# First modulation products of a two-block model on one Trainium2 core: four column quarters of the TensorE array, and the latent tokens' modulation ahead of the context's norm

## What is computed

```
def adaln(cvec, w, b):
    m = jax.nn.silu(cvec) @ w + b
    return jnp.split(m, 3, axis=-1)
...
sh_l, sc_l, gt_l = adaln(c, ada_w[i], ada_b[i])
h_lat = rms_norm(x_lat, norm_g[i]) * (1.0 + sc_l[:, None]) + sh_l[:, None]
...
sh_c, sc_c, gt_c = adaln(c_ctx, ada_w[i], ada_b[i])
h_ctx = rms_norm(x_ctx, norm_g[i]) * (1.0 + sc_c) + sh_c
...
y_lat, y_ctx = hgrn_mixer(h_ctx, h_lat, hg_w_in[j], lb, hg_norm_g[j], hg_w_out[j], ctx_out)
```

## Time and profile before

| | |
|---|---|
| median of 3 runs | 2519.7 us (2518.5 to 2519.74) |
| the profiled execution | 2521.25 us, span 2518.5 us |
| PE busy | 2461.1 us (98%) |
| DVE busy | 1633.3 us (65%) |
| ACT busy | 993.6 us (39%) |
| mean granted TensorE clock | 0.992 |

### The profile page before, as it was taken

One profiled execution on the slowest core, in us unless ns is written; L12 is line 12 of the kernel. 1 busy time (PEld: TensorE's weight loads), 2 busy tenths in 40 slices (PEclk: granted clock), 3 DMA queues, 4 the chain that ended last, 5 costly groups with the idle time before them and its releaser, 6 DMA issues.

```text
span 2518.5 us, 40380 instructions
## 1 busy us (share of the span) xinstructions
PE 2461.1 (98%) x14398; PEld 2147.0 (85%) x14398; DVE 1633.3 (65%) x2378; ACT 993.6 (39%) x1338; POOL 120.3 (5%) x138
## 2 busy tenths in 40 slices
PE   7999999999999998999999999989999999999998
PEld 2888888888888886888899999979999878888886
DVE  7567777777777775445555343468999975444346
ACT  4334444444444433333345222235455554322223
POOL 0011211111111100000000000000000000000000
PEclk9999999999999998999999999999999999999999
DMA  6212212122121232222222222222222222222222
GB/s 239 78 64 75 75 67 75 58 76 82 67 67 64 78 126 75 83 76 83 85 92 91 88 88 92 92 84 92 100 97 94 100 84 97 95 92 92 99 92 100
DMA packets 61983, 223.90 MB, mean 89 GB/s; under 512 B 6736, under 2 KB 8784, under 8 KB 61552
## 3 DMA queue, kind: packets, MB, share of 16 engines
q1 hardware_dynamic: 58992, 211.08, 24.7%
q0 software_dynamic: 2944, 12.19, 1.4%
HBM read 221.15 MB, written 2.10 MB: 89 GB/s over the span
## 4 chain that ended last, share of the span: by engine, by line
PE 93%; DVE 4%; ACT 1%; issue 1%; DMA 1%; ACTq 0%; DVEq 0%; SPq 0%
PE ps L489 81%; PE ps L663 4%; PE ps L685 1%; PE ps L546 1%; DMA ada_raw<-in_ada_weights_dram 1%; PE ps L676 1%; PE ps L704 1%; PE ps L650 1%; PE ps L695 1%; PE ps L696 1%; PE ps L697 1%; ACT w_hi L1060 1%; DVE w_lo L1603 1%; PE ps L633 0%; DVE n_sq L1622 0%
## 5 line engine op out<-in xcount | busy, mean ns | idle before, releaser
L1060 ACT ACTIVATE w_hi<-w_raw 128x1024 fp32r<-128x1024 f32 (+1 forms) x360 | 377.8, 1049 | 922.5 <-PE ps L489 913.7
L1603 DVE TENSOR_TENSOR w_lo<-w_raw,w_hi 128x1024 fp32r<-128x1024 f32 (+1 forms) x360 | 435.3, 1209 | 214.4 <-ACT w_hi L1060 212.2
L489 PE MATMUL ps<-n_hi,w_hi 128*128 128x512 f32 (+1 forms) x992 | 320.5, 355 | 11.9 <-DVE n_lo L1630 8.5
L489 PE MATMUL ps<-n_lo,w_hi 128*128 128x512 f32 (+1 forms) x992 | 319.6, 354 | 0.0
L489 PE MATMUL ps<-n_hi,w_lo 128*128 128x512 f32 (+1 forms) x992 | 318.0, 352 | 0.0
L489 PE MATMUL ps<-h_hi,w_hi 128*128 128x512 f32 x640 | 266.5, 416 | 4.8 <-DVE h_lo L1735 3.1
L489 PE MATMUL ps<-h_hi,w_lo 128*128 128x512 f32 x640 | 251.2, 393 | 0.0
L489 PE MATMUL ps<-h_lo,w_hi 128*128 128x512 f32 x640 | 250.4, 391 | 0.0
L489 PEld LDWEIGHTS ps<-n_hi,w_hi 128*128 128x128 f32 x992 | 174.5, 189 | 45.4 <-issue 11.0
L489 PEld LDWEIGHTS ps<-n_hi,w_lo 128*128 128x128 f32 x992 | 174.6, 189 | 25.9
L489 PEld LDWEIGHTS ps<-n_lo,w_hi 128*128 128x128 f32 x992 | 174.4, 189 | 26.1 <-issue 0.2
(11 more groups left out here) (367 smaller groups left out, 4963.8 us busy)
## 6 DMA issues: line engine op xcount, KB each, us to landing
w_raw<-in_weights_dram SPq DMA_DIRECT2D x376, 512.0 KB, 3.3
ada_raw<-in_ada_weights_dram SPq DMA_DIRECT2D x4, 2048.0 KB, 22.4
gate_raw<-in_gate_weights_dram POOLq DMA_DIRECT2D x16, 512.0 KB, 3.6
x<-in_x_dram SPq DMA_DIRECT2D x1, 2048.0 KB, 14.6
x<-in_x_dram POOLq DMA_DIRECT2D x1, 2048.0 KB, 9.9
out_dram<-fin SPq DMA_DIRECT2D x16, 128.0 KB, 1.9
xc<-in_ctx_dram SPq DMA_DIRECT2D x1, 1024.0 KB, 21.2
masks<-in_masks_dram POOLq DMA_DIRECT2D x1, 512.0 KB, 4.8
```

The costliest lines, as they stand in the source:

```text
L489: last = nc.tensor.matmul(o, w, xp, start=start and n == 0, stop=stop and n == 2)
L1060: run(w_hi[:, s, 0:n], w_raw[:, s, 0:n], ACT.Copy).then_inc(hi_ready[s], 1)
L1603: tt(w_lo[:, s, 0:n], w_raw[:, s, 0:n], w_hi[:, s, 0:n].bitcast(F32), ALU.subtract).then_inc(lo_ready[s], 1)
```

## The change

Each modulation matmul of 128x512 becomes four of 128x128. Each of the four takes one 128-column block of the weights, and its output lies in another quarter of the PSUM partitions (0, 32, 64, 96) and in another bank, which puts its two stationary columns into another quarter of the array's columns. The results of all four loads share the four banks, 128 columns each. ACT now copies twice: loads 0 to 2 together in four copies of 2x384, load 3 in four copies of 2x128. PE's products of load 3 wait for the first copy. On PE the latent tokens' `mean` stands behind load 0. On DVE `over_root(N0C, ...)` moves from ahead of the modulation to behind `first_lo` of the latent tokens, and `first_lo` now waits for the tiles of `over_root`.

```diff
+        QUAD = P // 4
...
             for n, (raw_, a, b_) in enumerate(ADA_LOADS):
                 pe.wait_ge(ada_loaded[n], 16)
+                if n == 3:
+                    pe.wait_ge(ada_copied, 1)
+
                 for k in range(KD):
-                    if n == 1 and k == KD - 2:
-                        mean(N0, T, st_sum[:, 0])
-                    last = nc.tensor.matmul(ps[0:2, n], csil[:, k], raw_[:, :, k * P:(k + 1) * P],
-                                            start=k == 0, stop=k == KD - 1)
+                    for q_ in range(4):
+                        last = nc.tensor.matmul(ps[q_ * QUAD:q_ * QUAD + 2, q_, n * P:(n + 1) * P], csil[:, k],
+                                                raw_[:, q_, k * P:(k + 1) * P], start=k == 0, stop=k == KD - 1)
                 last.then_inc(ada_part, 1)
+                if n == 0:
+                    mean(N0, T, st_sum[:, 0])
                 if n == 1:
                     mean(N0C, TC, st_sum[:, 1], bank=5)
             pe.wait_ge(ident_in_s, 16)
-            pe.wait_ge(ada_copied, 4)
+            pe.wait_ge(ada_copied, 2)
             for m_ in range(16):
-                last = nc.tensor.transpose(ps[:, 7, 2 * m_:2 * m_ + 2], ada_row[:, m_ // 4, tile_cols(m_ % 4)],
+                last = nc.tensor.transpose(ps[:, 7, 2 * m_:2 * m_ + 2], ada_row[:, m_ % 4, tile_cols(m_ // 4)],
                                            ident[0:2, 0:2])
...
-            def copy_ada(n):
-
-                act.wait_ge(ada_part, n + 1)
-                run(ada_row[:, n], ps[0:2, n], ACT.Copy).then_inc(ada_copied, 1)
-
-            copy_ada(0)
+            def copy_ada(first, end):
+
+                act.wait_ge(ada_part, end)
+                c = slice(first * P, end * P)
+                for q_ in range(4):
+                    last = run(ada_row[:, q_, c], ps[q_ * QUAD:q_ * QUAD + 2, q_, c], ACT.Copy)
+                last.then_inc(ada_copied, 1)
+
             act.wait_ge(xc_in_s, 16)
             squares(R0C, lambda k: xc[:, k], lambda k: st_tmpc[:, k % 2])
             root(N0, ps[:, 6], st_sq[:])
             root(N0C, ps[:, 5, 0:TC], st_tmpc[:, 2])
-            copy_ada(1)
+            copy_ada(0, 3)
             cut(0)
             cut(1)
-            copy_ada(2)
-            copy_ada(3)
+            copy_ada(3, 4)
...
             cut(0)
             cut(1)
-            over_root(N0C, xc, st_tmpc[:, 2])
 
             dve.wait_ge(ada_done, 1)
...
                         if k > 1:
                             dve.wait_ge(N["lo"], k - 1)
+                        dve.wait_ge(N["tmp"], k + 1)
...
             first_lo(N0, x0, 0, lambda k: st_tmp[:, k % 2], lambda k: h_hi[:, k], lambda k: h_lo[:, k])
+            over_root(N0C, xc, st_tmpc[:, 2])
             first_lo(N0C, xc, 1, lambda k: st_tmpc[:, k % 2], lambda k: hc_hi[:, k], lambda k: hc_lo[:, k])
```

## The result

The changed kernel takes 2522.88 us (median of 20 runs, 2520.99 to 2525.42), the kernel before 2519.3 us (20 runs, 2517.28 to 2519.8): ratio 1.0016, 95% interval 1.001 to 1.0023. It is slower by 3.6 us where a gain of 1.9 was forecast.

What follows compares the result with a forecast made beforehand. PE, 93% of the chain, was taken as the bound, so an earlier start ends the kernel earlier. Gain 43.63 - 41.7 = 1.9 us: 2521.25 to 2519.35 profiled, 2517.8 us median; range 2515.8 to 2522.5.

Steps and rivals of the forecast that it cites:

- Where the chain is read, and what the change cannot move: At the start: PE paces the rest; ACT's root stays at 29.17, DVE's cuts still end at 40.45.
- the floor for A: DVE's bias addition cannot come before about 40.4 us, when the cuts end; this limits the gain to 3.2 us.
- A: Time at which DVE adds the bias to the modulation: 46.12 us before, forecast 41.7.
- What A is worth: `project(2, "a")` starts no earlier than A + 21.69, against 65.32 before, so the gain is 43.63 - A.
- What A becomes: Loads, copies and transposes at full clock give A = 40.5; low clock 41.2 to 42.8; taken 41.7, gain 1.9 us.
- The step p: PE's time from one modulation pass to the next, taken as 0.055 us for partial overlap of quarters; a load is 64p.
- the 0.027 of the rival: Full overlap of four quarters in the modulation: step 0.027 us, gain 3.2, 2516.5 us; chance 0.26.
- It does not reach the end: Rival: a start earlier by 2 us is lost at a later DMA; chance 0.08 together with the clock rival below.
- no overlap: Rival: modulation quarters do not overlap, step 0.111 us, slower by 6.8 us, 2526.5; chance 0.15, including other causes above 0.1.
- The clock behind the context's products: Rival: PE's clock falls after `project(1, "c")`, losing 1.4 us; gain 0.5, 2519.2 us; chance 0.08 shared with a lost gain.

Runs made afterwards that it cites:

- e3: Kernel before with only DVE's new order and waits (context's norm behind the latent tokens' low parts): 2523.35 us, ratio 1.0021.
- e4: Changed kernel with DVE's order and waits as before, leaving quarters, copies and early mean: 2520.1 us, ratio 1.0009.
- e5: Changed kernel with 32 tiny filler matmuls behind load 0 on PE and one wait per `first_lo` instead of one per tile: 2517.22 us, ratio 0.9994.
- e10: Changed kernel with one wait per `first_lo` and 32 tiny filler matmuls behind load 2 on PE: 2516.35 us, ratio 0.9992.
- e1: Changed kernel with 32 tiny filler matmuls (128 instructions) on PE behind load 0: 2517.5 us, ratio 0.9999.
- e6: Kernel before with 12 one-column `memset` on DVE at the program's start: 2521.39 us, ratio 1.0011.
- e8: Changed kernel with one wait per `first_lo` instead of one per tile, no fillers: 2518.23 us, ratio 1.0002.
- e7: Kernel before with 64 tiny filler matmuls (256 instructions) ahead of PE's first product: 2519.36 us, ratio 1.0006.
- e12: Kernel before with 28 tiny filler matmuls (112 instructions) ahead of PE's first product: 2520.08 us, one run.
- e13: Kernel before with 30 tiny filler matmuls (120 instructions) ahead of PE's first product: 2519.09 us, one run.
- e9: e5 with the context's reciprocal ahead of the modulation on DVE, its eight products on GpSimd, and eight `memset` filling DVE's program: 2518.99 us, ratio 1.0001.
- e11: e10 with the context's reciprocal on DVE ahead of the modulation, its products still behind `first_lo`: 2515.18 us, ratio 0.9986.
- e2: Kernel before with 32 tiny filler matmuls (128 instructions) ahead of PE's first product: 2521.85 us, ratio 1.0016.

## Why the prediction was wrong

**Where the chain is read, and what the change cannot move:** right. The root follows the squares (27.86, 1.31 us earlier, as is the first square), and the floor for A stays.

**What A is worth:** right. The reciprocal of the context starts 9.83 us behind the bias addition (predicted 9.85), `project(1, "c")` starts at 56.75 (56.8), and `project(2, "a")` 21.60 behind the addition (21.69). e3, DVE's order alone, starts 2.4 us later; e4, the quarters alone, 1.3 earlier.

**What A becomes:** right in its result, wrong in two terms that offset each other. The step p was taken as 0.055; load 2 shows 64 passes in 1.93 us, 0.030 at full clock, so four quarters do overlap, near the 0.027 of the rival. At the lower level it is 3.59/64 = 0.056. The clock cost more than taken. Stretches of the changed kernel, with the granted clock before the last two numbers:

```profile
20.00:28.00 8.00, 5.67 (x67) 2.81 (x67) 5.28 (x11) 5.33 (x12) 0.68 (x1) 0.50 1.02 406
28.00:30.00 2.00, 2.00 (x54) 1.62 (x58) 1.42 (x1) 1.02 (x2) 0.00 (x0) 0.95 0.98 389
...
36.00:48.00 12.00, 7.16 (x32) 5.86 (x29) 10.34 (x20) 7.94 (x14) 0.00 (x0) 0.50 0.49 166
```

The transposes and the first head ran at the lower level too, and the copies took 1.97 and 1.11 instead of 1.63 and 0.75. A lies 1.3 us above the end of the cuts, as at 41.7 over 40.4; that it agrees so well is luck, since the step was taken nearly twice too long, and the clock and the copies too cheap. The start's gain is 2.0, forecast 1.9.

**It does not reach the end:** this step failed. The forecast rests on the sentence that whatever brings PE's run forward by a microsecond "ends the kernel a microsecond earlier, since all that follows is timed by PE". As a rival, the prediction said that a gain "could be lost at a later DMA. Weight blocks come by use and not by time, so I give this little". The DMAs that stand in PE's gap and in DVE's carry code, not weights, and whether an engine waits for them goes by the place of an instruction in the program. Each added instruction was costed where it runs, and none for what it does to the place of the code behind it. The profiled execution's sum: -3.17 at 92 us (of which -1.3 is the earlier landing), +1.13 and +1.44 for DVE's two gaps, +4.70 for PE's, +0.9 for the rest (of which 0.56 is a `mean` at 975 us that took 2.08 instead of 1.52 at another clock) give +5.0, the difference of the spans. With the three gaps taken away by length alone, the change gains 1.0 us in the median (e5, 0.9985 to 1.0003) and 2.2 (e10, 0.9983 to 1.0001), each against the kernel before of its own runs, where 1.9 was forecast; neither interval excludes that nothing is gained.

**The other rivals:** no overlap fell at once (0.030). The clock behind the context's products did not fall: `project(1, "c")` went at `hc_lo`'s pace, and the matmuls behind 62.04 step by 0.23.

**What stays open:** why a place 112 to 129 instructions further in a block misses and one 0 or 1 further does not. Whether the loop crosses a border may be what decides; a run with 60 or 190 instructions more, for which this forecasts no gap, could tell. It was not tried how far the good places reach. The medians do not split as cleanly as the traces: the two DVE gaps are worth 2.2 to 2.6 us in the traces, and 0.3 (e1 less e5), 3.2 (e6) and 3.5 us (after less e8, each against its own kernel before) in medians. Part of that is the clock, which differs between the traces: at 2000 us, behind a wait of 1.9 us for DVE, the matmuls of before and after ran at the lower level (0.72 granted from 2002 to 2008 in after) and those of e1, e3, e4, e6, e7, e8, e12 and e13 at the full one, worth 1.6 us. Traces with the same two lengths agree in it: e5, e9, e10 and e11 are all as slow there as before. So this too may go with the lengths; no run was made to test it.

## What to carry to other kernels

Count what a change adds in instructions for each engine, not only in time: code further down can miss its fetch, at the end of a loop above all, and a gain below 0.2% is easily eaten by it. A gap with no releaser but issue, at a place that the change did not touch, is the mark, and the test is cheap: pad the kernel before by the same number of instructions and see whether it slows as well. Compare versions at lengths without such gaps, and where a group of tiles is long done, wait once for it and not for each tile.

## What the hardware showed beyond that

- fp32 products of 128 columns in four column quarters step by 0.030 us a pass at full clock, though both passes of a matmul go to the same quarter; before, 32 passes of 512 columns took 13.84 us, 0.108 for each 128 columns.
- One operation's time on DVE rises from 0.69 to 1.22 and from 0.55 to 0.83 us while GpSimd multiplies 128x256 tiles (e9), and GpSimd itself takes 0.90 for a tile for which DVE takes 0.35.
- The clock level of PE behind an idle time of 2 to 3 us differs between kernels with the same work there: e12's fell for 3 us (0.57 granted from 1527 to 1530) behind a gap of 2.36, e2's stayed at 1.00 behind one of 2.70. One trace of each can't tell a difference of the kernels from one of the executions.
- Code arrives while the kernel runs, in packets of 16 KB (q8) and 8 KB (q14), and a wait for it shows as idle time with no releaser but issue.
